# Gate values of the returned rows: spread by four selection products behind the expert loop, in place of a trip through memory in 4-byte pieces

## The reference

```
top_val, top_idx = lax.top_k(logits, TOP_K)            # 4 experts for a token
gate = jax.nn.softmax(top_val, axis=-1)                # (512, 4)
# each expert e works on its tokens' rows:
#   y = clamped_swiglu(x @ w_e1[e] + b_e1[e]) @ w_e2[e] + b_e2[e]
y = zeros((T, D)).at[row_tok].add(y_rows * row_gate[:, None])
x = layer_norm(alpha * x + y)
```

## Time and profile before

| | |
|---|---|
| median of three executions | 1565.47 us (1564.57 to 1568.39) |
| profiled execution, first to last instruction | 1566.7 us |
| PE busy | 1414.7 us, 90% |
| DVE / ACT / POOL busy | 676.9 / 153.0 / 327.7 us |
| moved by DMA | 478.39 MB, mean 305 GB/s |
| granted TensorE clock, mean | 0.980 |

### The profile page before, as it was taken

One profiled execution on the slowest core, in us unless ns is written; L12 is line 12 of the kernel. 1 busy time (PEld: TensorE's weight loads), 2 busy tenths in 40 slices (PEclk: granted clock), 3 DMA queues, 4 the chain that ended last, 5 costly groups with the idle time before them and its releaser, 6 DMA issues.

```text
span 1566.7 us, 30023 instructions
## 1 busy us (share of the span) xinstructions
PE 1414.7 (90%) x12398; PEld 714.1 (46%) x12399; DVE 676.9 (43%) x1206; ACT 153.0 (10%) x283; POOL 327.7 (21%) x386
## 2 busy tenths in 40 slices
PE   7999999999999996999972988898689899999977
PEld 6887544468875632343330323333233333434432
DVE  5177443424425672344323543354344433434455
ACT  4112221211110020000000000000000000000001
POOL 1060000000000042333321432233223322323210
PEclk9999999999999997999996999999999999999999
DMA  6533000353335679999997999999999999999997
GB/s 222 191 110 119 10 0 1 100 149 94 95 119 230 248 297 422 403 423 421 420 418 303 414 419 424 423 423 422 423 424 422 423 423 425 423 425 421 422 394 269
DMA packets 100269, 478.39 MB, mean 305 GB/s; under 512 B 17380, under 2 KB 63876, under 8 KB 75272
## 3 DMA queue, kind: packets, MB, share of 16 engines
q1 hardware_dynamic: 83648, 457.68, 72.3%
q0 software_dynamic: 12080, 16.64, 2.9%
q10 hardware_dynamic: 4504, 3.57, 0.7%
HBM read 471.18 MB, written 23.09 MB: 315 GB/s over the span
## 4 chain that ended last, share of the span: by engine, by line
PE 69%; DMA 19%; issue 7%; DVE 4%; ACT 1%; POOL 0%; POOLq 0%; SPq 0%; DVEq 0%; ACTq 0%
PE ps L1906 24%; DMA big<-in_w_e 19%; PE ps L1932 12%; PE ps L1609 12%; PE ps L1776 4%; PE ps L1810 4%; PE ps L1597 3%; PE ps L1742 2%; PE ps L1753 2%; PE ps L1693 1%; PE ps L1711 1%; PE ps L1760 1%; DMA big<-expert_rows 1%; PE ps L1827 0%; DVE stat L1045 0%
## 5 line engine op out<-in xcount | busy, mean ns | idle before, releaser
L1906 PE MATMUL ps<-big,rest 128*32 128x512 f32 x5024 | 562.8, 602 | 103.7 <-DMA big<-in_w_e 47.4
L1906 PEld LDWEIGHTS ps<-big,rest 128*32 128x32 f32 x5024 | 163.2, 111 | 489.7 <-issue 488.7
L1932 PE MATMUL ps<-big,rest 128*32 128x256 f32 x5120 | 294.9, 380 | 23.6 <-DMA big<-in_w_e 18.8
L1932 PEld LDWEIGHTS ps<-big,rest 128*32 128x32 f32 x5120 | 177.1, 110 | 149.9 <-issue 43.1
L1450 DVE MEMSET stat<- 128x1 f32 x30 | 1.8, 59 | 422.2 <-PE ps L1906 422.2
L734 POOL DMA_INDIRECT rest<-x_rows,idx x120 | 147.5, 1230 | 57.2 <-issue 31.7
L750 POOL DMA_INDIRECT expert_rows<-rest,slot x120 | 119.5, 996 | 53.9 <-issue 28.3
L989 ACT ACTIVATE rest<-rest 128x1024 f32<-128x1024 f32 x32 | 33.9, 1059 | 910.9 <-DVE rest L1429 658.7
L742 POOL COPY idx<-P 128x4 uint32 (+1 forms) x30 | 5.6, 186 | 466.6 <-DVE rest L1451 458.0
L712 POOL IOTA P<- 128x128 f32 x1 | 0.2, 244 | 349.8 <-DVE rest L1277 349.8
L1609 PE MATMUL ps<-X,P 128*128 128x256 f32 x288 | 66.2, 379 | 0.0
(11 more groups left out here) (309 smaller groups left out, 1223.2 us busy)
## 6 DMA issues: line engine op xcount, KB each, us to landing
big<-in_w_e SPq DMA_DIRECT2D x189, 2048.0 KB, 25.5
rest<-in_w_in SPq DMA_DIRECT2D x14, 1024.0 KB, 5.1
big<-expert_rows SPq DMA_DIRECT2D x4, 2048.0 KB, 16.1
gate_area<-in_w_in SPq DMA_DIRECT2D x8, 512.0 KB, 4.6
rest<-in_w_in SPq DMA_DIRECT2D x8, 512.0 KB, 4.5
big<-in_w_out SPq DMA_DIRECT2D x1, 4096.0 KB, 13.3
X<-in_x SPq DMA_DIRECT2D x4, 512.0 KB, 9.2
h_rows<-X SPq DMA_DIRECT2D x1, 2048.0 KB, 7.6
```

Source lines behind the costliest of these rows:

```text
L1906: last = mm(ps[TB * g:TB * (g + 1), h0 + b, :], rows[:, k, b, :], w1, start=(k == 0), stop=(k == end))
L1932: last = mm(ps[TB * g:TB * (g + 1), 4 + b // 2, YW * (b % 2):YW * (b % 2 + 1)], acts[:, k, b, :], rows[:, k, YW * g:YW * (g + 1)], start=( ...
```

## The change

The load in 4-byte pieces and the store that it reads are gone. The store of `gatew`, which POOL's load near the end still reads, is issued ahead of the loop, as soon as DVE has the gates (`gatew_ready`). `main_rows` is made on chip: with `lane[p, t]` = 1 where p mod 32 is t, `to_rows[:, k]` holds `lane` in its columns 4 t + k and zeros elsewhere, and `own_gates` is `main_gate` with zeros where the partition is not in quarter c. The sum over k of `to_rows[:, k]` transposed times `own_gates[:, :, k, :]` is then `main_rows`, in PSUM bank 6, from where DVE copies it.

```diff
@@ SP: one semaphore for four row loads
-                    sp.dma_start(gain[:], A["ln1_g"].broadcast_to([P, D])).then_inc(ln1_landed, 16)
+                    sp.dma_start(gain[:], A["ln1_g"].broadcast_to([P, D])).then_inc(norm_rows_landed, 16)
@@ POOL, behind gather(2)
             step(nc.gpsimd.memset(no_rows, 0.0))
+            step(nc.gpsimd.memset(P1[:, SPREAD_AT:SPREAD_AT + TOPK * P], 0.0))
             nc.gpsimd.memset(last_gate, 0.0).then_inc(late_consts, 1)
...
-            pool.wait_ge(gates_stored, 32)
+            pool.wait_ge(gates_stored, 16)
@@ ACT
             act.activation(gatew[:], gatew[:], ACT.Exp).then_inc(router_exp, 1)
+            act.wait_ge(gatew_ready, 1)
+            act.dma_start(gates_dram.rearrange("(i p) k -> p i k", p=P), cut(gatew, 0, NT, TOPK)).then_inc(gates_stored, 16)
...
-            act.wait_ge(gates_ready, 1)
-            act.dma_start(gates_dram.rearrange("(i p) k -> p i k", p=P), cut(gatew, 0, NT, TOPK)).then_inc(gates_stored, 16)
-            act.dma_start(main_dram.rearrange("(i p) k -> p i k", p=P), cut(main_gate, 0, NT, TOPK)).then_inc(gates_stored, 16)
             act.wait_ge(x1_stored, 16 * NT)
...
-            with act.Fori(1, E // 4) as it:
-                turn(it)
-            act.wait_ge(gates_stored, 32)
-            act.dma_start(main_rows.rearrange("p (j a) -> p j a", a=1),
-                          main_dram.rearrange("(j t) (k a) -> (t k) j a", t=TB, a=1), allow_slow_non_contiguous=True).then_inc(main_landed, 16)
-            with act.Fori(E // 4, n_it) as it:
+            with act.Fori(1, n_it) as it:
                 turn(it)
@@ DVE
-            step(nc.vector.tensor_tensor(gw, gw, gs.broadcast_to([P, NT, TOPK]), ALU.mult))
+            nc.vector.tensor_tensor(gw, gw, gs.broadcast_to([P, NT, TOPK]), ALU.mult).then_inc(gatew_ready, 1)
@@ DVE, gates_of_late_rows
-                nc.vector.tensor_tensor(main_gate, main_gate, gatew[:], ALU.mult).then_inc(gates_ready, 1)
+                dve.wait_ge(gatew_ready, 1)
+                step(nc.vector.tensor_tensor(main_gate, main_gate, gatew[:], ALU.mult))
+                step(nc.vector.tensor_reduce(lane.rearrange("p (t a) -> p t a", a=1), ident[:].rearrange("p (c t) -> p t c", c=CG), X_AXIS, ALU.add))
+                dve.wait_ge(late_consts, 1)
+                for k in range(TOPK):
+                    step(nc.vector.tensor_copy(to_rows[:, k, :, k], lane))
...
+                for c in range(CG):
+                    own = nc.vector.tensor_scalar(own_gates[:, :, :, c], cut(main_gate, 0, NT, TOPK), own_block[:, c:c + 1], None, ALU.mult)
+                    if c == CG - 1:
+                        own.then_inc(gate_parts, 1)
+                    else:
+                        step(own)
@@ DVE, late_selections
-                dve.wait_ge(main_landed, 16)
+                dve.wait_ge(main_spread, 1)
+                step(nc.vector.tensor_copy(main_rows, ps[:, 6, 0:NQ]))
@@ PE, behind the loop
+            pe.wait_ge(gate_parts, 1)
+            for k in range(TOPK):
+                last = mm(ps[:, 6, 0:NQ].rearrange("p (i c) -> p i c", c=CG), to_rows[:, k].rearrange("p t k -> p (t k)"), own_gates[:, :, k, :],
+                          start=(k == 0), stop=(k == TOPK - 1))
+            last.then_inc(main_spread, 1)
             pe.wait_ge(aT_turned, n_it)
             pe.wait_ge(y_ready, n_it)
             fc2(last_blocks, last_w2_landed, 16, acts=last_aT, rows=last_W2)
             pe.wait_ge(x1_scaled, 1)
+            pe.wait_ge(row_gates, 1)
             residual(2)
```

More of the change, by code:

```diff
@@ L87, in build_program @@
     gates_dram = nc.dram_tensor("gates", (S, TOPK), F32, kind="Internal").ap()
-    main_dram = nc.dram_tensor("main_gates", (S, TOPK), F32, kind="Internal").ap()
     gate_of_row = gates_dram.rearrange("t (k a) -> (t k) a", a=1)
@@ L320, in build_program @@
         fourth = hn[:, S + YW:S + YW + TB]
+        to_rows = cut(P1, SPREAD_AT, TOPK, TB, TOPK)
+        lane = P1[:, FLOAT_AT:FLOAT_AT + TB]
+        own_gates = cut(P1, FLOAT_AT + TB, NT, TOPK, CG)
         SMALL_AT = 16
@@ L452, in build_program @@
         last_w2_landed = [sem(f"last_w2_landed{u}") for u in range(W2_UNITS)]
-        gates_ready = sem("gates_ready")
+        gatew_ready = sem("gatew_ready")
         gates_stored = sem("gates_stored")
-        main_landed = sem("main_landed")
+        gate_parts = sem("gate_parts")
+        main_spread = sem("main_spread")
         late_consts = sem("late_consts")
@@ L467, in build_program @@
         centred = sem("centred")
-        ln2_landed = sem("ln2_landed")
-        ln1_landed = sem("ln1_landed")
+        norm_rows_landed = sem("norm_rows_landed")
         out_ready = sem("out_ready")
@@ L537, in _ @@
                 if n == 5:
-                    sp.dma_start(gain[:], A["ln1_g"].broadcast_to([P, D])).then_inc(ln1_landed, 16)
-                    sp.dma_start(bias[:], A["ln1_b"].broadcast_to([P, D])).then_inc(ln1_landed, 16)
+                    sp.dma_start(gain[:], A["ln1_g"].broadcast_to([P, D])).then_inc(norm_rows_landed, 16)
+                    sp.dma_start(bias[:], A["ln1_b"].broadcast_to([P, D])).then_inc(norm_rows_landed, 16)
                 if n == 5:
@@ L995, in _ @@
             glu_sigmoid(1)
-            act.dma_start(gain[:], A["ln2_g"].broadcast_to([P, D])).then_inc(ln2_landed, 16)
-            act.dma_start(bias[:], A["ln2_b"].broadcast_to([P, D])).then_inc(ln2_landed, 16)
-            act.wait_ge(gates_ready, 1)
-            act.dma_start(gates_dram.rearrange("(i p) k -> p i k", p=P), cut(gatew, 0, NT, TOPK)).then_inc(gates_stored, 16)
-            act.dma_start(main_dram.rearrange("(i p) k -> p i k", p=P), cut(main_gate, 0, NT, TOPK)).then_inc(gates_stored, 16)
+            act.dma_start(gain[:], A["ln2_g"].broadcast_to([P, D])).then_inc(norm_rows_landed, 16)
+            act.dma_start(bias[:], A["ln2_b"].broadcast_to([P, D])).then_inc(norm_rows_landed, 16)
             act.wait_ge(x1_stored, 16 * NT)
@@ L1362, in layer_norm_1 @@
                 layer_norm_scale(NORM1 + i, t, x1_ready)
-            dve.wait_ge(ln1_landed, 32)
+            dve.wait_ge(norm_rows_landed, 32)
             dve.wait_ge(router_landed, 32)
@@ L1530, in _ @@
             move_late_rows(1)
-            dve.wait_ge(ln2_landed, 32)
+            dve.wait_ge(norm_rows_landed, 64)
             def norm_2_center(i):
```

## The result

The changed kernel took 1552.92 us (median of four executions, 1552.24 to 1557.87); beside it the kernel before took 1565.02 (1564.51 to 1568.39). The ratio is 0.9928 [0.9916, 0.994], 12.1 us less. The forecast was 1551.3 us, faster.

What follows compares the result with a forecast made beforehand. DMA was taken to bound the loop, at 423 GB/s of weights. 11.7 + 1.7 + 1.2 - 0.3 - 0.1 = 14.2 us off the profiled span of 1566.7, less 1.2 to the median, gave 1551.3 us, range 1548.5 to 1557.6.

Steps and rivals of the forecast that it cites:

- the bias was not held up by the pieces: Rival for the loop: something else delays DVE's bias spread, so the wait stays; 1565.5 us, no change, chance 0.05.
- One piece for one weight run: On the DMA engines in the loop, each small piece lets one 16 KB weight run pass, 0.62 us.
- the packet rule: Engines switch queues every 9 to 17 descriptors; the prediction took 128 pieces to need only 5 to 9 us, against 78.9 traced.
- the hole, not the wait: In the loop, a wait of PE or DVE costs only the DMA rate lost when queues run dry, not its length.
- Removed load, 11.7 us: Dropping the 4-byte load closes the rate hole between 848 and 863 us: gain 11.7 us, bounds about 6 to 11.7.
- Stores, 1.7 us: Removing one store and moving the other closes the rate dip from 630 to 640 us: gain 1.7, from 0 to 1.7.
- The pieces themselves, 1.2 us: Beside the pieces, from 570 to 615 and 768 to 847 us, the rate is 419, not 423 GB/s: gain 1.2 us.
- The store in its new place, 0.3: Ahead of the loop, the moved store may hold up the x1 rows by 0 to 1.6 us; 0.3 us taken as cost.
- DVE, 2.5 us and 0: Nine more DVE instructions take 2.5 us and delay the next expert's work by 0.4 us; nothing is paid.
- PE's products, 1.1 us and 0.1: Behind the loop, four products take about 1.06 us; 0 to 1.1 stick out, 0 to 0.5 is paid, 0.1 taken.
- the 2.6 us that I named: Sign of being wrong: PE's wait before the last expert's second product exceeds 2.6 us.
- Sum: Gains 11.7, 1.7 and 1.2 less costs 0.3 and 0.1 give 14.2 us off the whole kernel; likeliest case, chance 0.80.

Runs made afterwards that it cites:

- full: Changed kernel with the load of 2048 4-byte pieces put back after the seventh turn, into a tile nobody reads: 1564.43 us, 0.9998 of the kernel before.
- quarters: Kernel before, stores and all 2048 load pieces kept, the load cut into four parts of 512 with a loop turn between them: 1555.61 us, ratio 0.9943.
- half: Changed kernel with a load of 1024 4-byte pieces put back after the seventh turn, read by nobody: 1556.31 us, 0.9947 of the kernel before.
- double: Changed kernel with two loads of 2048 4-byte pieces, one behind the other, after the seventh turn: 1571.17 us, 1.0044 of the kernel before.
- before_again: The kernel before, timed and profiled a second time without any edit: 1565.1 us, ratio 0.9998.
- stores_late: Changed kernel with both 16-byte-piece stores issued where the kernel before had them, still without the 4-byte load: 1555.35 us, 0.993 of the kernel before.
- wide: Changed kernel with the same 8 KB loaded after the seventh turn as 128 pieces of 64 bytes: 1556.67 us, 0.9947 of the kernel before.
- no_products: Changed kernel without the selection products, their DVE instructions and the POOL memset, output wrong: 1552.49 us, 0.992 of the kernel before.
- warm4: Changed kernel with the opening products of tile 2 alone made twice (4 more instructions) in PE's idle tail: 1554.14 us, 0.993 of the kernel before.
- after_again: The changed kernel, timed and profiled a second time without any edit: 1555.82 us, 0.9939 of the kernel before.
- split: Changed kernel with only ACT's loop cut in two after the seventh turn, nothing in between: 1555.77 us, 0.9937 of the kernel before.
- warm: Changed kernel with the opening products of tiles 2 and 0 made twice (8 more instructions) in PE's idle tail: 1555.95 us, 0.9942 of the kernel before.

## Why the prediction was right, and which of its terms were not

**The mechanism: shown.** Biases behind pieces in one queue make DVE late, DVE makes PE late, PE frees no buffer, and the DMA queues run dry. With the pieces gone the waits and the holes are gone; with the load back, the long wait and its hole are back (full); with the load spread out, they are gone and the pieces still move (quarters). The rival "the bias was not held up by the pieces" is refuted by the same three.

**One piece for one weight run: borne out roughly, as a mean.** Pieces on an engine and landing: 26.2 us for 32, 42.8 for 64 (half), 78.7 for 128 (full). That is 0.82, 0.67 and 0.61 us for each, not one number; from half to full the 64 pieces more took 35.9 us, 0.56 each, which is 0.9 of the 0.62 us of a weight run, and some 7 us come on top whatever the count. With the weight queues empty (the store at 553.5 us in the changed kernel) 32 pieces landed in 3.0 us, in the predicted 2 to 5. double adds the counter-test: its first 2048 pieces landed at 761.7 + 78.5 = 840.2 us, the second 2048 at 762.1 + 87.3 = 849.4, only 9.2 us later, and in these the weights ran out (199 GB/s from 846 to 847 us, 9 from 848 to 849).

What the prediction worked out from the packet rule of the Trainium skill ("DMA: Bandwidth & Descriptors", section on queues, rings and completion order) does not follow from it. It let each turn of 9 to 17 pieces pass one weight run. If the weight runs too go by 9 to 17 at a turn, 128 pieces let some 128 runs pass, and the rule gives the 79 us of the trace. So the 78.9 us do not speak against the rule, and the rule gives the rival "the bias was not held up by the pieces" no ground.

**The measure "the hole, not the wait": right, and it has a rule.** The same window, 840 to 866 us, gives for each kernel the wait of `spread_b1` and the full rate that is lost, 26 x (1 - rate/423):

| kernel | wait of DVE | GB/s | lost | wait less lost |
|---|---|---|---|---|
| before, first profile | 48.77 | 232 | 11.7 us | 37.1 |
| before_again | 46.79 | 257 | 10.2 | 36.6 |
| full | 44.62 | 300 | 7.6 | 37.0 |
| stores_late, first gap | 25.10 | full | 0 | |
| half | 8.91 | 422 | 0 | |

At this place of the loop the first 37 us or so of the wait are free, and each one beyond costs one; three points, all between 44 and 49 us, give that number, and half's wait, at the same place, agrees with it. What the reserve is made of is not measured. double does not fit as well: its 43.76 + 11.61 us of wait less the 15.2 us lost (175 GB/s) are 40.2. And 37 us is no number of the whole loop: at the first gap the reserve is smaller, as the stores show.

**Removed load, 11.7 us: right in kind, too large in size.** The rule says why: it was read off an execution with a wait of 48.77, and 2 to 4 us less wait is 2 to 4 us less loss. By before_again it is 10.2, by full 7.6. Over many executions full (0.9998) against half and wide (0.9947 both) gives 8 us for it, pieces included. One thing is left over: full has a smaller hole than both profiles of before, by 2.6 and 4.1 us, and the same time; what it loses elsewhere is not found.

**Stores, 1.7 us: there in that one execution, nothing in the others.** The traces tell how the hole from 630 to 640 us came about. In the first profile of before PE stood 14.81 us and began again at 621.00 us, in before_again 11.60 us and 619.81, in stores_late 11.86 and 619.40, in quarters 11.05 and 619.06. The clock was at its lower level behind the idle, and it came back later too. The stretch from 620 to 625 us, in the first profile and in before_again:

```profile
620.00:625.00 5.00, 4.00 (x20) 0.99 (x24) 4.70 (x8) 0.22 (x1) 3.59 (x4) 0.50 1.02 428
```

```profile
620.00:625.00 5.00, 5.00 (x36) 1.19 (x34) 4.77 (x8) 0.00 (x0) 2.96 (x4) 0.73 1.01 418
```

From 625 to 630 us it was 0.81 and 1.00 (1.00 in stores_late and quarters too). So PE freed its first weight buffer late, and SP issued the next load at 630.34 us, where the others have 626.33 to 626.82:

```profile
630.34 14.89 SPq L578 DMA_DIRECT2D big<-in_w_e  x4
```

The step was right that the hole follows from the first gap. It failed in taking the hole of one execution for one of the kernel: with waits of DVE of 24.55 to 25.10 us no rate is lost (before_again, stores_late, quarters), with 27.30 us 1.7 us are. By the measure above the reserve of this gap is therefore about 25.6 us, and the waits of the other three traces lie just within it. That the later restart and the slower clock together made the hole is read from these four traces; no run changes one of them alone.

**The pieces themselves, 1.2 us: three quarters of it.** In 768 to 847 us 419 became 424, and quarters, with the pieces, stays at 419: 79 x 5/424 = 0.9 us. In 570 to 615 us nothing changed (419 to 418), so the stores' share was not theirs.

**The store in its new place, 0.3: borne out as small.** PE's transposes of the first x1 rows began at 556.72 us, before 557, and were at 556.54 before the change.

**DVE, 2.5 us and 0: right.** The nine instructions took 0.38 + 0.90 + 1.27 = 2.55 us; `turn_x` began at 575.93 in place of 575.41, 0.5 us later for a forecast of 0.4; the DMA rate beside it did not move.

**PE's products, 1.1 us and 0.1: right in duration, open in price.** Eight instructions, 1.07 us, and PE waited no more than 0.49 for DVE behind them, far below the 2.6 us that I named. But behind the last wait for weights the changed kernel's profile spent 3.1 us more than that of before. Two things make them up: the last scatter took 4.08 us to land in place of 2.07, partly made good by row loads of 8.54 in place of 9.14; and the clock fell, 1.65 us. Neither was in the sum, and no rival priced them. The clock fell in before_again too, and in 8 of the 14 profiles in all (5.5 us for the two pieces each time), so it is no property of the change; the scatter stays open (below).

**Sum.** For the profiled pair the parts up to the last wait for weights came to 13.95 us for a sum of 14.2: the hole of 11.7, the 1.7 of that execution's first hole and 0.9 for the pieces make 14.3, of which 0.2 go to PE's later start (556.72 for 556.54 us). The tail took 3.3 back. For the medians, 9.7 to 12.1 us were measured. The prediction also set a span beside times: it put the profiled execution 1.2 us above the median, but its time was 1568.39 us, 2.9 above, and so it was taken for more usual than it was. That the time came out within 1.6 us (1552.92 for 1551.3) is in part luck: the load term was about 2 us too large, the store term of 1.7 us is not there in the usual execution, the tail was not in the sum, and the changed kernel's level was 3 us better at its first timing than at its second, by which the gain of 14.2 us is 4.5 too large.

**What stays open.** The last scatter lands in 2.07 to 2.11 us in before, before_again, quarters, no_products and warm4, and in 3.7 to 4.2 in after, after_again, split, stores_late, full, half, wide, double and warm. The first four have no products, but warm4 has them. In the first pair it makes 1.4 us, since the rows behind it then load faster. Over the profiles it decides less: from the start of this landing to the first product with the returned rows 10.5 to 12.2 us pass in before, before_again, quarters and no_products, and 11.8 to 12.8 in those with the longer scatter (warm left out). I have no cause for it. Nor do I know why the first weights of the loop flow at 232 to 318 GB/s from 561 to 570 us, from one profile to the next, which is 9 x 86/423 = 1.8 us of full rate; part of the 3 us between the two timings of the changed kernel may be that. And no run puts the pieces on a queue that carries no bias.

## What to carry to other kernels

A small transfer of many small pieces costs by its number of pieces in a row on a queue whose other members are waited for. Count them per DMA engine, multiply by the time of a piece beside the other transfers (here 0.6 to 0.8 us), see how long that makes the engine behind wait, and compare with the reserve that the queues have at that place (here 37 us at one gap and some 25.6 at another): below it the pieces are nearly free, beyond it every microsecond is paid. Then the cheapest cure may be to cut the transfer into parts between the turns of the loop, which here was worth as much as replacing it by computation. And before a hole in one profile is priced as a term, see whether a second execution has it.

## What the runs showed of the hardware that was not expected

- A transfer that waits behind many pieces blocks the engine that issues it, not only the queue. The issue of a bias took 0.5 us in an ordinary turn, 18.45 us in the earlier trace rows, 11.89 in full, 45.58 in double, and the second load of double 37.01. In double ACT's next sigmoid was late by it. Before, before_again, full and double have in common that the first issue that was held returned 37.4 to 39.1 us after the issue of the 2048 pieces. In half, with 1024 pieces and the next issue 26 us behind them, nothing was held (0.56 us).
- The page of the Trainium skill on "DMA: Bandwidth & Descriptors" (section on queues, rings and completion order) has engines turn between queues by packets of typically 9 to 17 descriptors. Here pieces and 16 KB runs passed nearly one for one on the mean (0.56 us a piece from 64 to 128 pieces an engine), and at a rate that stayed at 417 to 424 GB/s. Equal turns of any size would give that, so these runs neither confirm nor refute the page's figure.
- Idle of PE of 2.6 to 3.6 us in the tail was sometimes followed by a lower granted clock (0.75 in after, 5.5 us for two pieces) and sometimes not: after_again had 2.59 us of idle and no_products 2.91, the clock stayed at 1.00, and the same two pieces took 3.85.
